# Depthwise convolution in a fused model kernel: seven of the 31 taps multiplied on ScalarE and summed on GpSimd

## The reference

```python
D_CONV = 1024; CONV_WIDTH = 31
def _conformer_conv_mixer(glu_in, conv_w, conv_b, ln_g, ln_b):
    u = glu_in[..., :D_CONV] * jax.nn.sigmoid(glu_in[..., D_CONV:])
    u = lax.conv_general_dilated(
        u, conv_w[:, None, :], window_strides=(1,), padding=((CONV_WIDTH - 1, 0),),
        dimension_numbers=('NWC', 'WIO', 'NWC'), feature_group_count=D_CONV) + conv_b
    u = _layernorm(u, ln_g, ln_b)
    return jax.nn.silu(u)
...
c_out = _conformer_conv_mixer(glu_in, conv_w[l], conv_b[l], conv_ln_g[l], conv_ln_b[l])
gates = jax.nn.sigmoid(gate_logits).reshape(b, t, N_BRANCHES, D_MODEL)
merged = gates[:, :, 0] * (a_out @ w_rwkv_proj[l]) + gates[:, :, 1] * (c_out @ w_conv_proj[l])
```

## Time and profile before

| | |
|---|---|
| median of 3 runs | 2711.13 us (2708.30 to 2712.52) |
| profiled execution: time, span | 2708.64 us, 2706.8 us |
| TensorE matmul busy | 2552.1 us, 94% |
| VectorE busy | 1366.5 us, 50% |
| ScalarE busy | 889.5 us, 33% |
| GpSimd busy | 1126.6 us, 42% |
| mean granted TensorE clock | 0.978 of full speed |
| convolution loop | from about 1986 to 2192 us of the span |

### The profile page before, as it was taken

One profiled execution on the slowest core, in us unless ns is written; L12 is line 12 of the kernel. 1 busy time (PEld: TensorE's weight loads), 2 busy tenths in 40 slices (PEclk: granted clock), 3 DMA queues, 4 the chain that ended last, 5 costly groups with the idle time before them and its releaser, 6 DMA issues.

```text
span 2706.8 us, 46961 instructions
## 1 busy us (share of the span) xinstructions
PE 2552.1 (94%) x18466; PEld 2075.7 (77%) x18466; DVE 1366.5 (50%) x2022; ACT 889.5 (33%) x1420; POOL 1126.6 (42%) x659
## 2 busy tenths in 40 slices
PE   8788899999899998999998899999999988999998
PEld 6565688887687876888876688888887767788886
DVE  3554873355504258553367655666669963321112
ACT  4323422223623334222244333333333334332231
POOL 4433554444544445444443423232334335444442
PEclk9899999999999999999998899999999999999999
DMA  4410222222220212322222111111122212232231
GB/s 156 94 40 17 85 94 97 98 93 94 78 94 24 71 48 79 100 93 97 98 73 73 56 34 39 43 41 34 34 74 92 83 57 91 88 100 94 94 101 54
DMA packets 56624, 203.19 MB, mean 75 GB/s; under 512 B 6800, under 2 KB 7480, under 8 KB 56464
## 3 DMA queue, kind: packets, MB, share of 16 engines
q1 hardware_dynamic: 54288, 196.37, 21.9%
q0 software_dynamic: 1344, 3.68, 0.8%
q10 hardware_dynamic: 832, 0.82, 0.1%
HBM read 197.17 MB, written 3.67 MB: 74 GB/s over the span
## 4 chain that ended last, share of the span: by engine, by line
PE 79%; DVE 9%; issue 4%; ACT 4%; POOL 2%; DMA 2%; DVEq 0%; SPq 0%; ACTq 0%; POOLq 0%
PE banks L1845 21%; PE banks L1846 21%; PE banks L1847 21%; PE banks L2298 9%; DMA bias_rows<-sb_brow 1%; PE banks L2348 1%; PE banks L2064 1%; DVE banks L1632 1%; ACT sb_pa L639 1%; PE banks L2047 1%; POOL sb_pa L1719 1%; DVE sb_x L1100 1%; PE banks L1978 1%; PE banks L2026 1%; PE banks L2022 1%
## 5 line engine op out<-in xcount | busy, mean ns | idle before, releaser
L1692 POOL TENSOR_TENSOR sb_wl<-sb_raw,sb_wh 128x1024 fp32r<-128x1024 f32 (+1 forms) x366 | 885.7, 2423 | 1154.9 <-ACT sb_wh L458 1154.6
L1845 PE MATMUL banks<-sb_bh,sb_wh 128*128 128x512 f32 x2656 | 1060.5, 399 | 77.5 <-POOL sb_bl L1705 26.6
L1846 PE MATMUL banks<-sb_bl,sb_wh 128*128 128x512 f32 x2656 | 1045.7, 394 | 0.0
L1847 PE MATMUL banks<-sb_bh,sb_wl 128*128 128x512 f32 x2656 | 1044.5, 393 | 0.0
L1845 PEld LDWEIGHTS banks<-sb_bh,sb_wh 128*128 128x128 f32 x2656 | 504.3, 190 | 210.9 <-issue 52.8
L1847 PEld LDWEIGHTS banks<-sb_bh,sb_wl 128*128 128x128 f32 x2656 | 504.1, 190 | 110.1
L1846 PEld LDWEIGHTS banks<-sb_bl,sb_wh 128*128 128x128 f32 x2656 | 504.7, 190 | 107.2 <-issue 2.4
L458 ACT CAST sb_wh<-sb_raw 128x1024 fp32r<-128x1024 f32 (+1 forms) x366 | 376.8, 1032 | 535.2 <-PE banks L1847 530.7
L1020 DVE SCALAR_TENSOR_TENSOR sb_x<-sb_x,banks 128x512 f32 x72 | 49.5, 688 | 315.0 <-PE banks L1847 315.0
L2298 PEld LDWEIGHTS banks<-sb_m 64*64 64x64 f32 x5632 | 195.4, 134 | 16.5 <-issue 8.1
L2298 PE MATMUL banks<-sb_m 64*64 64x64 f32 (+1 forms) x5632 | 206.4, 229 | 0.5 <-DVE sb_w L1533 0.2
(11 more groups left out here) (332 smaller groups left out, 2589.6 us busy)
## 6 DMA issues: line engine op xcount, KB each, us to landing
sb_raw<-w SPq DMA_DIRECT2D x366, 512.0 KB, 3.4
sb_x<-xT SPq DMA_DIRECT2D x4, 512.0 KB, 6.7
out<-sb_x SPq DMA_DIRECT2D x4, 512.0 KB, 2.7
bias_rows<-sb_brow POOLq DMA_DIRECT2D x1, 1536.0 KB, 36.6
sb_pj<-pT POOLq DMA_DIRECT2D x2, 512.0 KB, 4.0
sb_t<-bias_rows POOLq DMA_DIRECT2D x1, 512.0 KB, 4.2
sb_sq<-bias_rows POOLq DMA_DIRECT2D x1, 512.0 KB, 4.8
sb_wm<-wm ACTq DMA_DIRECT2D x1, 288.0 KB, 3.0
```

The costliest lines, as they stand in the source:

```text
L1692: nc.gpsimd.tensor_tensor(wl[:, s, 0:cols], raw[:, s, 0:cols], wh[:, s, 0:cols].bitcast(F32), ALU.subtract).then_inc(lo_ready, 1)
L1845: nc.tensor.matmul(out, hi_a, hi_b, start=first, stop=False)
L1846: nc.tensor.matmul(out, hi_a, lo_b, start=False, stop=False)
L1847: return nc.tensor.matmul(out, lo_a, hi_b, start=False, stop=last)
```

## The change

Taps 24 to 30 leave VectorE. ScalarE multiplies them one by one, `Identity` with a scale column of `cw`, into seven slots: `s1`, `s1c`, `sd`, `rs`, the second half of `t2`, and then `s1c` and `sd` once more. Two are made at step 1, two at step 2, three at step 3, behind the step's cast and ahead of its sigmoid. GpSimd adds the six later ones to `s1`, one at step 1, two at step 2, three at step 3, behind the step's low part. VectorE adds `s1` to bank 4 behind tap 23, which now writes into `t2`. The taps of the second half are 16 to 23.

Two semaphores are new: `tap_ready` from ScalarE to GpSimd, and `tap_used` from GpSimd to ScalarE (a slot is free), to GpSimd itself (the sum is written) and to VectorE (all six are in). At step 1 ScalarE waits until the gated product has freed its bank, that is, until `ub` is written.

```diff
-CHUNK_LINKS = 33
+CHUNK_LINKS = 27
+DVE_TAPS = 24
...
+        tap_slots = [s1, s1c, sd, rs, t2[:, 1, :], s1c, sd]
...
+        tap_ready, tap_used = sem("tap_ready"), sem("tap_used")
...
+            def late_taps(c, some):
+                for i in some:
+                    if i > 4:
+                        act.wait_ge(tap_used, c * 6 + (i - 4))
+                    tap = DVE_TAPS + i
+                    nc.scalar.activation(tap_slots[i], ub[:, tap:tap + T], ACT.Identity,
+                                         scale=cw[:, c, tap:tap + 1]).then_inc(tap_ready, 1)
+
             def sigmoid(j, p, b):
 
+                if j.k == 1:
+                    act.wait_ge(bank_free[b], (j + g0).over2() + 1)
+                if j.k:
+                    late_taps(j.turn, {1: (0, 1), 2: (2, 3), 3: (4, 5, 6)}[j.k])
                 if j.k % 2 == 0:
...
-                        dst = t2[:, 0, :] if tap == 29 else acc
+                        dst = t2[:, 0, :] if tap == DVE_TAPS - 1 else acc
...
-                        if tap == 30:
+                        if tap == DVE_TAPS - 1:
                             link(ins)
...
                 gated(3, mg[:, c, :], 1)
-                taps(range(16, 31))
+                taps(range(16, DVE_TAPS))
+                dve.wait_ge(tap_used, c * 6 + 6)
+                link(V.tensor_tensor(psum[:, 4, :], psum[:, 4, :], s1, ALU.add))
                 link(V.tensor_tensor(y[:, c, :], psum[:, 4, :], t2[:, 0, :], ALU.add))
...
-            panels(4 * NC)
+            p0 = w.p
+
+            def late_taps(j):
+                low(j + (p0 + 3))
+                c = j.turn
+                for i in {0: (), 1: (1,), 2: (2, 3), 3: (4, 5, 6)}[j.k]:
+                    pool.wait_ge(tap_ready, c * 7 + (i + 1))
+                    if i > 1:
+                        pool.wait_ge(tap_used, c * 6 + (i - 1))
+                    nc.gpsimd.tensor_tensor(s1, s1, tap_slots[i], ALU.add).then_inc(tap_used, 1)
+            turns(pool, 4 * NC, late_taps)
+            w.p += 4 * NC
             panels(5)
```

## The result

| | before | after |
|---|---|---|
| median, four runs each on one chip | 2711.82 us (2708.30 to 2712.77) | 2686.16 us (2684.69 to 2687.97) |
| ratio, 95% interval | | 0.9908 (0.9891 to 0.9925) |
| span of the profiled execution | 2706.8 us | 2683.1 us |

The change made the kernel 25.7 us faster, 0.9%; 2687.1 was forecast, in a range from 2682.5 to 2697.0. The two profiled executions differ by 23.7 us, where the sum had 24.0.

A forecast was written before the change was run, and what follows sets the result against it. VectorE was taken to set the loop's pace at 24.45 us a turn, TensorE's floor being 21.76. 22.0 us at the mean plus 2.0 us of clock made 24.0: 2711.1 - 24.0 = 2687.1 us, range 2682.5 to 2697.

The forecast's parts named there:

- The floor: Convolution loop: TensorE's own pace when not held, 21.76 us a turn, 2.69 us under the present 24.45.
- The dip of the clock at 2146: TensorE's lower clock level in the loop: costs nothing in the kernel before, since VectorE covers it, and won't occur.
- VectorE's turn: Convolution loop: seven multiply-adds go (4.62 us), one addition comes (0.73), so 24.45 falls to 20.56 us.
- The slack of 1.2 us: Convolution loop: VectorE's turn of 20.56 us would be 1.2 us less than TensorE's 21.76.
- ScalarE: Seven multiplications add 4.3 us a turn to 8 us of work; cost nothing, cover 2.5 us at the nearest place.
- GpSimd, the mis-sized term: Six additions at 1.15 us with four low parts make 16.5 us a turn; chain ends at 13.9, slack 3.8 us.
- Ports: VectorE beside GpSimd: multiply-adds and the new addition have one input in PSUM, so no contention was taken.
- rival 3: Taps 0 to 23 and GpSimd's additions block each other: 27.2 us a turn, 22 us slower, 2733; chance 3%.
- The stage's end and the clock: Mean at line 1950 starts 22.0 us earlier; without the low clock, the step to the sums of squares saves 2.0 us.
- rival 2: Loop's end and normalisation: low clock returns at about 2 us each, or waits eat VectorE's slack; 2691 to 2697; chance 15%.
- Rival 1: GpSimd's sum comes late to VectorE in the loop: turns of 22.3 to 23.3 us, 2702; chance 7%.
- rival 4: Convolution loop: TensorE wasn't bound by VectorE, so time wouldn't move; 1%.

The follow-up runs named there:

- the runs with 26 and 28 taps: Changed kernel with only five (26 on VectorE) or three taps (28) moved to ScalarE and GpSimd instead of seven: 2689.01 us and 2702.12 us.
- The runs with the SBUF accumulator: VectorE's odd taps collected in SBUF tile t2 instead of a PSUM bank: 2743.71 us on the changed kernel, 2746.72 us on the kernel before.
- the kernel with the late mean: Changed kernel plus ten unread VectorE additions between the loop and the copy that the mean waits for: 2694.20 us, ratio 0.9944.

## Why the prediction was right

**The floor.** 21.76 us a turn was read from two sigmoids of ScalarE and came to the hundredth. Leaving out four more taps did not lower it, nor did taking the work off the helpers, and TensorE waits for nothing in the loop: it is TensorE's. The dip of the clock at 2146 that was to go is gone; the level is 1.00 through the whole loop of after.

**VectorE's turn.** 20.56 us was worked out, 20.66 follows from the runs with 26 and 28 taps. The new addition takes 0.70 us, forecast by the row of the same operand kinds. The slack of 1.2 us was 1.1: of the 1.70 us of idle time 0.62 is what VectorE always shows between turns.

**ScalarE.** Two taps take 1.34 us, and the three at step 3 1.94 with their overlap, and the sigmoid (L982) comes 5.51 us behind the opening product, on time. TensorE waited for ScalarE nowhere in the loop.

**GpSimd, the mis-sized term.** The additions were put at 1.15 us, between 1.06 (line 1798) and 1.27 to 1.34 (line 1705). The line of after (min/median/max):

```profile
L1853 POOL TENSOR_TENSOR sb_w<-sb_w x40: 1287/1297/1316, 1998.7 to 2162.4; 128x512 f32<-128x512 f32 x40
```

1.30 us and 1.34 from start to start: the upper bound was the right row, and 1.15 lay nearer the lower one, chosen for its output type. Six such additions put the chain's end at 14.9 us behind the opening product instead of 13.9, and the slack at 2.9 us instead of 3.8. This cost nothing, but the margin was two additions, not three.

**Ports.** The 168 multiply-adds took 749 ns in the mean and 756 at most beside both kinds of work on GpSimd. The runs with the SBUF accumulator show the other branch: 28.9 us a turn with eleven exposed taps, where rival 3 had 27.2 for six held ones.

**The stage's end and the clock.** 22.0 us were forecast for line 1950 and 22.2 came; 2.0 for the step from there to the sums of squares, and 2.1 came. That the level hangs on TensorE's wait there is shown by the kernel with the late mean, in which 1.8 of it are lost again.

**What wasn't in the sum.** The 1.4 us given back in the normalisation is rival 2's mechanism, at a new place (2228.5 to 2231.8) and for less than the 2 us that it had for each return. The sum took everything behind the loop to go as before, but the low stretches there shifted against the wait for GpSimd. The first opening product came 1.0 us earlier for a reason ahead of the loop, where nothing was changed. In the other profiled execution of the same kernel it stood at 1998.88. The two nearly cancel, so the agreement of 23.7 with 24.0 is partly luck; the loop up to the mean and the step behind it, 22.2 and 2.1 against 22.0 and 2.0, stand by themselves.

**The rivals.** Rival 1 needed four more additions to appear (turns of 23.3 us, as the rival had them; that 2702.92 meets its 2702 is partly chance, since the profiled execution has 4.1 us ahead of the loop). Rival 2 came in a small part, rival 3 only with another accumulator. Rival 4, that TensorE wasn't bound by VectorE, is excluded by the five- and three-tap runs.

## What to carry to other kernels

Before work is taken off the engine that sets a loop's pace, read the next engine's own pace from a turn in which it was not held: here that floor, 2.7 us under the present turn, fixed the gain. Moving five taps won 22.8 us, moving seven 25.7, and leaving out eleven no more than seven. An idle engine is a free helper only as long as the two don't hold each other up: here, keep the other engine's accumulators in PSUM, and look at the operand places before the durations. Behind the loop, count a wait of TensorE together with the clock level that follows it, and ask where the next low stretch will fall.

## What the runs showed of the hardware

- A multiply-add with two SBUF inputs slowed from 739 ns at best to 1510 in the mean and 2634 at most beside GpSimd, while GpSimd's additions went from 1298 to 1572 ns. Both engines lose.
- Tap 1, a tensor_scalar, took 477 ns from SBUF to SBUF and 745 from SBUF to a bank. In the kernel before with odd taps in SBUF one of eight took 2072 ns, and it is the only one of them that ran beside a low part on GpSimd. In the kernel before, the form that writes a bank ran beside a low part in seven of eight turns and took 745 ns at most. So here the faster form is the one that was held up, on one row. This line is from that kernel (min/median/max):

```profile
L1630 DVE TENSOR_SCALAR sb_t<-sb_ub,sb_cw x8: 477/479/2072, 1998.0 to 2203.8; 128x512 f32<-128x512 f32 x8
```

- A float32 addition of 128x512 on GpSimd takes 1.30 us with two SBUF tiles of the full size; line 1798, which gave the lower bound, had 1.06, but it is a multiplication, and its second operand is eight columns, each read 64 times. Which of the two makes it quicker wasn't tried.
